# Memory keys before the tokens, four-tile lag matrices, later U loads and re-split convolution taps in a two-layer hybrid decoder step

## The chip, the cores and the metric

The kernel runs on one core of a Trainium2 chip. The metric is the device time of one execution in microseconds (us), lower is better. The engines are TensorE (PE), VectorE (DVE), ScalarE (ACT), GpSimd (POOL) and SyncE (SP, whose queue issues most loads).

## The reference

One inference step of a two-layer trunk on 512 prompt positions and 8 single-token samples, width 1024. Each layer normalises the residual, makes one input projection and runs three branches from it: a diagonal complex state-space branch, a causal depthwise convolution of 31 taps, and a 4-head cross-attention to 256 memory tokens (the samples attend to cached keys and values of their own). Gates merge the branches, and an output projection is added to the residual.

```python
def mixer_layer(x, s0_re, s0_im, conv_buf, mk, mv, p):
    h = rmsnorm(x, p['norm_g'])
    u_a, z_a, u_b, z_b, q, z_x, g_a, g_b, g_x = jnp.split(h @ p['w_in'], IN_SPLITS, axis=-1)
    y_a, s_new = s5_branch(u_a, s0, ...)          # state-space scan over positions
    o_a = (glu(gelu(y_a)) * jax.nn.silu(z_a)) @ p['w_br_ssm']
    v_b = u_b[..., :E_CONV] * jax.nn.sigmoid(u_b[..., E_CONV:])
    c_b, buf_new = causal_depthwise_conv(v_b, conv_buf, p['conv_w'], p['conv_b'])
    o_b = (silu(layernorm(c_b)) * jax.nn.silu(z_b)) @ p['w_br_conv']
    prob = jax.nn.softmax(q @ mk / sqrt(128))     # mk, mv = rmsnorm(mem) @ w_k, @ w_v
    o_x = (prob @ mv * jax.nn.silu(z_x)) @ p['w_br_xatt']
    m = sigmoid(g_a) * o_a + sigmoid(g_b) * o_b + sigmoid(g_x) * o_x
    return x + m @ p['w_out'], ...
```

## The kernel before

Everything is kept with channels on partitions: tokens are 2 groups of 260 columns (256 prompt and 4 samples). Each engine runs one instruction stream written out by hand, and semaphores alone order the work between them; a DMA stands in the queue of the engine that issues it, in program order.

**Projections.** A weight of 128 output channels arrives in two halves of 256 KB (`w_st`, loaded by SP in a fixed order). ACT casts each half to a rounded high word `w_hi`, POOL subtracts to get the low word `w_lo` (L615), and PE adds three products for each piece (`split_product`, L723): high by high, high by low, low by high. The residual is split in the same way into `h_hi` and `h_lo` by DVE and ACT at the start of each layer (the split chain, L1594 and around). The unit names are v (convolution input and gate), q, u, e (gates and the like), x (gate of the attention branch), b, a.

**Start of a layer.** `first_pair` makes the two v0 tiles; `key_values(first, end)` makes the memory's keys (0 to 3) and values (4 to 7) from `memg`, the memory tokens times the norm's gain, in quarters of the contraction. In layer 0 the tokens and memory rows arrive with tokens on partitions and PE transposes them; the row factor of the norm is spread by a product with ones (`rs`). The memory norm there runs inside the split chain. In layer 1 the square sums of the new residual give `rs`.

**DVE's taps.** `convolution(i, first, end)` runs taps `first` to `end` of channel tile i as one instruction each (L1459, `cacc<-vx,cw,cacc`); a tile starts when POOL has multiplied its gate (L627, L629). The order of these calls among DVE's other work is written out by hand:

```python
convolution(0, 0, TAPS)
convolution(1, 0, 23)
...
convolution(3, 10, TAPS)
wait(dve, l, "oxT_tr", 1)
```

**Middle of a layer.** On PE: `lag_matrices(0)` (L946, products of powers that give the state-space kernel's lags), `sample_products(0)` (L906: the samples' probabilities psT with cached values), the x1 pair, `sample_products(1)`, half of e3, `turn_sample` (the sample outputs, turned from the copy `oxs` that ACT makes), half of e3, `turn_inputs(0)`, and so on to `outputs(1)` (L958, L965). ACT copies the turned psT (L1307) after the gate of x0. SP loads U, the state-space inputs re-laid through memory, with 12 DMAs between x1's two weights. `keep_lags` copies the lag products out (`kt`), `take_inputs` and `scan` run the state recurrence on DVE, `output_matrices` makes the next V.

## Time and profile before

| | us |
|---|---|
| three runs | 1156.16, 1157.31, 1158.66 (median 1157.31) |
| profiled execution | 1154.06 |
| its span | 1152.3 |
| PE busy | 1086.5 (94%) |
| DVE busy | 813.7 (71%) |
| POOL busy | 460.0 (40%) |
| PE idle before the first q product, layers 0 and 1 | 2.85 and 6.14 |
| PE idle before the sample products, layers 0 and 1 | 5.08 and 5.42 |

A busy PE is not PE at its peak, and an engine's idle time costs only where it ends on the chain that sets the end. A timeline row gives the start in the span, the duration of the group of equal neighbours, the operation with its tiles and how many instructions it holds, and in brackets the idle time before it with what ended it.

### The profile page before, as it was taken

Reading aid. Unit: us, or ns where it says so; the run is one execution under the profiler, and the core shown is the slowest. Engines: PE = TensorE matmul, PEld = TensorE weight load, DVE = VectorE, ACT = ScalarE, POOL = GpSimd, SP = SyncE. Lnnn points to the kernel's source line nnn. Section 1 sums busy time; section 2 is a strip of 40 time slices with the busy share of each in tenths; the row PEclk is TensorE's granted clock in tenths of the full one; section 3 lists DMA queues with packets and bytes.
Section 4 is the critical chain, followed back from the end, with each engine's and each line's share of the span. In section 5 each row is a group of like instructions: output and inputs, shape, how many; then the busy total and the mean of one; then the engine's idle time right before and its main releaser. Section 6 shows DMA issues by size and latency. Waiting matters only on the chain.

```text
span 1152.3 us, 20452 instructions
## 1 busy us (share of the span) xinstructions
PE 1086.5 (94%) x8274; PEld 1015.4 (88%) x8274; DVE 813.7 (71%) x1209; ACT 419.4 (36%) x714; POOL 460.0 (40%) x329
## 2 busy tenths in 40 slices
PE   3999999989999999999989799998999999999995
PEld 3658998969999999999956799896999999999994
DVE  4868888998966784444489888989996867644412
ACT  4612553324453342222433245322444445222222
POOL 2037544454433224444313845445443322444440
PEclk8899999989999999999999899999999999999997
DMA  7235516784416723445432453478432564334422
GB/s 218 80 122 153 205 56 202 193 177 115 130 56 139 200 98 120 129 129 164 138 109 75 112 202 101 137 230 180 131 115 79 115 150 153 120 122 135 131 84 74
DMA packets 225300, 155.01 MB, mean 135 GB/s; under 512 B 48690, under 2 KB 201706, under 8 KB 223142
## 3 DMA queue, kind: packets, MB, share of 16 engines
q1 hardware_dynamic: 220454, 144.14, 44.8%
q10 hardware_dynamic: 4752, 9.57, 2.3%
q8 instruction: 65, 1.06, 0.4%
q14 instruction: 29, 0.24, 0.1%
HBM read 130.38 MB, written 24.24 MB: 134 GB/s over the span
## 4 chain that ended last, share of the span: by engine, by line
PE 66%; DVE 16%; DMA 5%; SPq 2%; POOL 2%; ACT 2%; issue 1%; DVEq 0%; ACTq 0%
PE acc L723 41%; PE mp L1059 12%; DVE cacc L1459 6%; PE mp L764 3%; PE acc L1040 2%; POOL w_lo L615 2%; DMA w_st<-in_w_in 2%; PE mp L664 2%; PE mp L935 1%; PE mp L826 1%; PE mp L864 1%; DMA y_scratch<-U 1%; DVE V L1453 1%; SPq L510 1%; DVE X L1453 1%
## 5 line engine op out<-in xcount | busy, mean ns | idle before, releaser
L615 POOL TENSOR_TENSOR w_lo<-w_st,w_hi 128x512 fp32r<-128x512 f32 x288 | 439.8, 1532 | 592.7 <-ACT w_hi L1145 592.1
L1145 ACT CAST w_hi<-w_st 128x512 fp32r<-128x512 f32 x288 | 177.4, 620 | 564.3 <-PE acc L723 370.4
L723 PE MATMUL acc<-h_hi,w_hi 128*128 128x260 f32 x1600 | 329.4, 287 | 10.0 <-POOL w_lo L615 9.0
L723 PE MATMUL acc<-h_lo,w_hi 128*128 128x260 f32 x1600 | 322.5, 283 | 0.0
L723 PE MATMUL acc<-h_hi,w_lo 128*128 128x260 f32 x1600 | 321.9, 283 | 0.0
L723 PEld LDWEIGHTS acc<-h_hi,w_hi 128*128 128x128 f32 x1600 | 247.6, 189 | 20.4 <-issue 18.1
L723 PEld LDWEIGHTS acc<-h_hi,w_lo 128*128 128x128 f32 x1600 | 247.0, 189 | 0.0
L723 PEld LDWEIGHTS acc<-h_lo,w_hi 128*128 128x128 f32 x1600 | 246.8, 189 | 0.0
L1459 DVE SCALAR_TENSOR_TENSOR cacc<-vx,cw,cacc 128x512 f32<-128x512 f32 x232 | 192.8, 902 | 1.5
L1059 PE MATMUL mp<-br_hi,w_hi 128*128 128x260 f32 x384 | 77.4, 283 | 4.7 <-POOL w_lo L615 4.7
L1059 PE MATMUL mp<-br_lo,w_hi 128*128 128x260 f32 x384 | 77.3, 283 | 0.0
L1059 PE MATMUL mp<-br_hi,w_lo 128*128 128x260 f32 x384 | 77.2, 283 | 0.0
L1453 DVE TENSOR_TENSOR mj<-mp,xT 128x520 f32<-128x520 f32 x16 | 11.2, 699 | 77.0 <-PE mp L1059 75.7
L1059 PEld LDWEIGHTS mp<-br_hi,w_hi 128*128 128x128 f32 x384 | 59.0, 188 | 5.0 <-issue 5.0
L764 PE MATMUL mp<-wkv,memg 128*128 128x512 f32 x128 | 57.5, 599 | 2.8 <-DMA wkv<-in_w_v 1.2
L1059 PEld LDWEIGHTS mp<-br_hi,w_lo 128*128 128x128 f32 x384 | 59.3, 188 | 0.0
L1059 PEld LDWEIGHTS mp<-br_lo,w_hi 128*128 128x128 f32 x384 | 59.2, 189 | 0.0
L764 PEld LDWEIGHTS mp<-wkv,memg 128*128 128x128 f32 x128 | 23.4, 190 | 34.4 <-issue 26.5
L1453 DVE TENSOR_TENSOR xT<-acc,xT 128x520 f32<-128x520 f32 x16 | 11.2, 700 | 59.4 <-PE acc L723 59.4
L1453 DVE TENSOR_TENSOR X<-X,s 128x16 f32<-128x16 f32 (+9 forms) x88 | 49.8, 566 | 3.0
L723 PE MATMUL acc<-m_hi,w_hi 128*128 128x260 f32 x256 | 51.6, 283 | 0.0
L723 PE MATMUL acc<-m_lo,w_hi 128*128 128x260 f32 x256 | 51.6, 283 | 0.0
(300 smaller groups left out, 1447.6 us busy)
## 6 DMA issues: line engine op xcount, KB each, us to landing
w_st<-in_w_in SPq DMA_DIRECT2D x208, 256.0 KB, 3.3
g_scratch<-xT ACTq DMA_DIRECT2D x32, 260.0 KB, 2.7
xT<-g_scratch SPq DMA_DIRECT2D x8, 1040.0 KB, 7.0
kb<-in_cache_mem_k SPq DMA_DIRECT2D x16, 512.0 KB, 5.3
kb<-in_cache_mem_v SPq DMA_DIRECT2D x16, 512.0 KB, 4.9
w_st<-in_w_out SPq DMA_DIRECT2D x32, 256.0 KB, 2.8
x_scratch<-xT SPq DMA_DIRECT2D x2, 2080.0 KB, 7.5
xT<-x_scratch SPq DMA_DIRECT2D x4, 1040.0 KB, 6.1
```

The costliest lines, as they stand in the source:

```text
L510: sp.dma_start(yg[:, :, t // 4, (t % 4) * C:(t % 4 + 1) * C], Ug[t * H:(t + 1) * H, :, NB:YC]).then_inc(sm["y_out"], 16)
L615: pool.tensor_tensor(w_lo[:, slot, :], w_st[:, slot, :], w_hi[:, slot, :].bitcast(F32), ALU.subtract).then_inc(w_staged_free, 1)
L664: return pe.transpose(out, in_, ident[0:n, 0:n])
L723: last = pe.matmul(acc_ps[pair][:, a, 0:HC], w[:, slot, kk * P:(kk + 1) * P], x[:, k, a, :], start=(k == 0 and p == 0), stop=(k == KT - 1 ...
L764: last = pe.matmul(mp[:, 2 * (1 - i // 4) + m, :], memg[:, k, m * P:(m + 1) * P], wkv[:, i % 2, kk * E:(kk + 1) * E], start=(k == 0), stop ...
L826: last = pe.matmul(mp[:, 2 * (i % 2) + hd // 2, (hd % 2) * MEM:(hd % 2 + 1) * MEM], q[:, hd, i // 2, (i % 2) * P:(i % 2 + 1) * P], kT[:, h ...
L864: last = pe.matmul(mp[:, hd, :], vtok[:, m, hd * P:(hd + 1) * P], pT[:, hd, m, :], start=(m == 0), stop=(m == 1))
L1040: last = pe.matmul(acc_ps[j][:, a, 0:HC], w_dir[:, g, k * 2 * P + j * P:k * 2 * P + (j + 1) * P], u[:, k, a, :], start=(k == 0), stop=(k = ...
L1059: last = pe.matmul(mp[:, 2 * jj + a, 0:HC], w[:, slot, c0:c0 + P], y[:, x, k, a, :], start=(k == 0 and i == 0), stop=(k == ET - 1 and i == 2))
L1145: act.copy(w_hi[:, c % SLOTS, :], w_st[:, c % SLOTS, :]).then_inc(w_hi_done, 1)
L1453: run(dve.tensor_tensor(out, a, b, op), behind)
L1459: run(dve.scalar_tensor_tensor(out=out, in0=a, scalar=s, in1=b, op0=op0, op1=op1), behind)
```

## The change

It has five parts. (1) In layer 0 ACT's queue issues the memory rows and two key weights before anything else; PE transposes the raw memory, DVE multiplies it by the gain out of PSUM, and PE makes the key products 0 to 3 between the token transposes. The memory's row factor is applied when ACT copies keys and values out. DVE's step factors move to before the split chain. (2) In layer 1, one key product stands before the square sums instead of two, and parameter steps move one output tile earlier, the first powers (1, 2) into the output tiles and level 4 behind the split chain. (3) The lag matrices go to four 32-column tiles of PE, and `kt`, `dt`, `eye` and `dcol` take the matching shape. (4) SP loads x1's and e3's weights and the cached values 4 to 7 before U; ACT copies psT before the second half of x0's gate. (5) The taps are split at other places, with 19 taps of tile 3 between `output_matrices(1)` and `take_inputs(1)`.

```diff
 
-                if l == 0:
-                    pair("v0")
-                    sp.dma_start(mrow[:, :, :], mem_prompt[0].rearrange("(m p) d -> p m d", p=P)).then_inc(sm["mem_in"], 16)
-                    state_loads(0)
+                if l:
                     kv_load(0)
                     kv_load(1)
-                else:
-                    kv_load(0)
-                    kv_load(1)
-                    pair("v0")
+                pair("v0")
+                if l == 0:
+                    state_loads(0)
+                    kv_load(2)
+                    kv_load(3)
                 pair("v1")
...
+                for i in range(2 if l else 4, 6):
                     kv_load(i)
-                if l:
-                    half("q0", 0)
+                half("q0", 0)
                 kv_load(6)
-                if l:
-                    half("q0", 1)
+                half("q0", 1)
                 kv_load(7)
-                if l == 0:
-                    pair("q0")
                 half("q1", 0)
...
                     wait(sp, l, "kq_done", b + 5)
                     cache_load(cache_mem_v, b)
                 half("x1", 0)
+                half("x1", 1)
+                half("e3", 0)
+                for b in range(4, NB):
+                    wait(sp, l, "pvs_done", b - 3)
+                    cache_load(cache_mem_v, b)
...
@@ -465,18 +465,13 @@
                 for a in range(2):
                     sp.dma_start(Ug[0:H, :, 4 * a:4 * a + 4], ug[:, :, a, 4 * C:HC]).then_inc(sm["U_in"], 16)
                     sp.dma_start(Ug[7 * H:P, :, YC + 4 * a:YC + 4 * a + 4], ug[:, :, a, 4 * C:HC]).then_inc(sm["U_in"], 16)
-                half("x1", 1)
-                half("e3", 0)
-                for b in range(4, NB):
-                    wait(sp, l, "pvs_done", b - 3)
-                    cache_load(cache_mem_v, b)
 
...
+            def memory_turns(j):
+
+                pe.wait_ge(sm["mem_in"], 32)
+                for k in range(HK):
+                    for m in range(2):
+                        last = transpose(acc_ps[j][:, k // 2, (k % 2) * MEM + m * P:(k % 2) * MEM + (m + 1) * P],
+                                         mrow[:, m, (HK * j + k) * P:(HK * j + k + 1) * P], P)
+                last.then_inc(sm["x_tr"], 1)
...
@@ -786,17 +790,23 @@
                     last.then_inc(sm["par_tr"], 1)
 
                 if l == 0:
+                    key_values(0, 1)
+                    token_turns(0)
+                    token_turns(1)
+                    sample_turns()
+                    key_values(1, 2)
+                    token_turns(2)
+                    token_turns(3)
+                    key_values(2, 3)
+                    row_factors()
+                    key_values(3, 4)
                     pe.wait_ge(sm["x_ev"], 5)
-                    state_turns()
-                    first_pair()
-                    pe.wait_ge(sm["mem_ev"], 2)
-                    key_values(0, 4)
                 else:
-                    key_values(0, 2)
+                    key_values(0, 1)
                     square_sums()
-                    key_values(2, 4)
-                    state_turns()
-                    first_pair()
...
                         pe.sem_inc(entered, 1)
-                    for r in range(QH):
+                    for g in range(2):
                         for ri in range(2):
-                            last = pe.matmul(mp[0:2 * H, r // 4, (r % 4) * P:(r % 4 + 1) * P],
-                                             bd[:, ri, f * QH + r, :, :].rearrange("p e h -> p (e h)"),
-                                             V[:, ri, r, 0:T, :].rearrange("p t h -> p (t h)"),
-                                             start=(ri == 0), stop=(ri == 1))
+                            for j in range(4):
+                                r = 4 * g + j
+                                last = pe.matmul(mp[32 * j:32 * j + 32, 0, g * P:(g + 1) * P],
+                                                 bd[:, ri, f * QH + r, :, :].rearrange("p e h -> p (e h)"),
+                                                 V[:, ri, r, 0:T, :].rearrange("p t h -> p (t h)"),
+                                                 start=(ri == 0), stop=(ri == 1), tile_position=(0, 32 * j))
                     last.then_inc(sm["k_done"], 1)
 
...
-                    if j == 4 and l + 1 < LAYERS:
+                    if j == 3 and l + 1 < LAYERS:
                         param_turns(l + 1)
 
...
+            for m in range(2):
+                act.dma_start(mrow[:, m, :], mem_prompt[0, m * P:(m + 1) * P, :]).then_inc(sm["mem_in"], 16)
+            for i in range(2):
+                act.dma_start(wkv[:, i, :].rearrange("p (k c) -> p k c", c=E),
+                              w_k[0].rearrange("(k p) c -> p k c", p=P)[:, 2 * i:2 * i + 2, :]).then_inc(d_loaded[i], 16)
             exponents(0)
-            sines(0)
...
+            act.wait_ge(sm["mem_in"], 32)
+            for m in range(2):
+                row_squares(P, mrow[:, m, :], 5 + m)
+            for j in range(2):
+                wait(act, 0, "memg_done", HK * (j + 1))
+                act.copy(memn[:, HK * j:HK * (j + 1), :].rearrange("p k m -> p (k m)"),
+                         acc_ps[j][:, :, :].rearrange("p b c -> p (b c)")).then_inc(sm["mem_ev"], 1)
+            act.wait_ge(sm["mem_ev"], 2)
+            act.dma_start(m_dram, memn[:, :, :].rearrange("p k m -> p (k m)")).then_inc(sm["mem_out"], 16)
             for i in range(4):
...
                     wait(act, l, "kv_used", 4)
                     if l == 0:
                         act.wait_ge(sm["mem_out"], 16)
-                    act.copy(ktok[:, :, :], mp[:, 2:4, :]).then_inc(sm["kv_ev"], 1)
-
-                if l:
-                    keep_keys()
+                    for m in range(2):
+                        last = act.activation(ktok[:, m, :], mp[:, 2 + m, :], ACT.Copy, scale=stat[:, 56 + m:57 + m])
+                    last.then_inc(sm["kv_ev"], 1)
...
                 act.activation(ps[:, :], mp[0:32, 0, 0:MEM], ACT.Exp, bias=stat[0:32, 48:49], scale=SCALE,
                                accum_out=stat[0:32, 49:50]).then_inc(sm["exps_done"], 1)
                 one("x0", 0, to_z(2))
-                one("x0", 1, to_z(2))
+                ready(1, use["x0"], unit["x0"] + 1)
                 wait(act, l, "psT_tr", 1)
                 wait(act, l, "psT_clear", 1)
                 act.copy(psT[:, :, :, 0:16], mp[:, 3, 0:64].rearrange("p (m g c) -> p m g c", m=2, g=2)).then_inc(sm["psT_ev"], 1)
...
                     if l + 1 < LAYERS:
                         square(j)
+                        if j == 3:
+                            exponents(l + 1)
                         if j == 4:
-                            exponents(l + 1)
+                            sines(l + 1)
                         if j == 5:
...
+            for j in range(2):
+                dve.wait_ge(sm["x_tr"], j + 1)
+                dve.tensor_tensor(memg[:, HK * j:HK * (j + 1), :], acc_ps[j][:, :, :].rearrange("p b (k m) -> p (b k) m", m=MEM),
+                                  vec[:, 56 + HK * j:56 + HK * (j + 1)].unsqueeze(2).to_broadcast([P, HK, MEM]),
+                                  ALU.mult).then_inc(sm["memg_done"], HK)
             angles(0)
...
             dve.sem_inc(sm["dg_done"], 1)
+            step_factors(0)
...
 
-                if l == 0:
-                    step_factors(0)
-                    first_powers()
+                first_powers((1, 2, 4) if l == 0 else (4,))
                 chunk_powers()
...
                         tt(cv[:, i, 0, :, 0:4 * C], even, odd, ALU.add)
 
                 convolution(0, 0, TAPS)
-                convolution(1, 0, 23)
+                convolution(1, 0, 14)
                 scores_max(0)
                 wait(dve, l, "qrow_ev", 2)
                 tt(qrow[32:32 + NB, :], qraw[:, :], qrow[0:NB, :].bitcast(F32), ALU.subtract)
                 dve.sem_inc(sm["qlo_done"], 1)
-                convolution(1, 23, 28)
+                convolution(1, 14, 19)
                 scores_max(1)
                 probabilities(0)
-                convolution(1, 28, TAPS)
+                convolution(1, 19, 23)
                 probabilities(1)
 
                 wait(dve, l, "b_in", 64)
...
+                convolution(1, 23, 27)
                 probabilities(3)
 
...
-                    run(dve.tensor_copy(kt[:, :, :].rearrange("h q x -> h (q x)"), mp[0:2 * H, 0:2, :].rearrange("h b x -> h (b x)")))
+                    run(dve.tensor_copy(kt[:, :, :].rearrange("h q x -> h (q x)"), mp[:, 0, 0:2 * P]))
...
                 wait(dve, l, "kv_out", 32)
                 input_matrices(0)
-                convolution(2, 3, 19)
+                convolution(1, 27, TAPS)
+                convolution(2, 0, 12)
...
                 output_matrices(0)
-                convolution(2, 19, 22)
+                convolution(2, 12, 15)
...
                 dve.tensor_scalar(ps[:, :], ps[:, :], stat[0:32, 51:52], None, ALU.mult).then_inc(sm["ps_norm"], 1)
-                convolution(2, 22, TAPS)
-                convolution(3, 0, 10)
+                convolution(2, 15, 21)
                 keep_lags(0)
-                convolution(3, 10, TAPS)
+                convolution(2, 21, TAPS)
+                convolution(3, 0, 8)
                 wait(dve, l, "oxT_tr", 1)
                 for hd in range(HEADS):
                     run(dve.tensor_copy(q[:, hd, :, 4 * C:HC], mp[:, 0:2, hd * (P + 1):hd * (P + 1) + 109:36]))
                 dve.sem_inc(sm["ox_done"], 1)
+                convolution(3, 8, 12)
...
                 output_matrices(1)
+                convolution(3, 12, TAPS)
                 take_inputs(1)
                 scan(1, lambda: keep_lags(1))
...
                             add_square(l, j - 1)
+                        if j == 2:
+                            step_rows(l + 1)
                         if j == 3:
-                            step_rows(l + 1)
+                            columns(l + 1)
                         if j == 4:
-                            columns(l + 1)
+                            angles(l + 1)
                         if j == 5:
-                            angles(l + 1)
+                            step_factors(l + 1)
                         if j == 6:
-                            step_factors(l + 1)
+                            first_powers((1, 2))
                 dve.sem_inc(sm["x_full"], 1)
                 if l + 1 < LAYERS:
                     add_square(l, KT - 1)
                     dve.sem_inc(sm["sq_sum"], 1)
-                    first_powers()
```

## Rows read from the trace of the kernel before

**Rows 1.** The page: busy time of the engines, and the chain that ended last.

```profile
PE 1086.5 (94%) x8274; PEld 1015.4 (88%) x8274; DVE 813.7 (71%) x1209; ACT 419.4 (36%) x714; POOL 460.0 (40%) x329
...
PE 66%; DVE 16%; DMA 5%; SPq 2%; POOL 2%; ACT 2%; issue 1%; DVEq 0%; ACTq 0%
```

**Rows 2.** PE's timeline in layer 0: start us, duration us, what, [idle before <- its releaser].

```profile
24.29 2.05 PE L694 MATMUL mp<-dg,ones 128*128 128x128 f32 x8 [4.55 <-DVEq L1571]
...
48.41 7.11 PE L764 MATMUL mp<-wkv,memg 128*128 128x512 f32 x16 [0.37 <-ACT memg L1098]
...
93.59 0.48 PE L723 MATMUL acc<-h_hi,w_hi 128*128 128x260 f32 x2 [2.85 <-POOL w_lo L615]
```

**Rows 3.** PE's timeline at the start of layer 1.

```profile
598.40 0.77 PE L749 MATMUL acc<-h_hi,w_hi 128*128 128x260 f32 x2 [2.61 <-DVEq L1594]
...
645.44 0.77 PE L723 MATMUL acc<-h_hi,w_hi 128*128 128x260 f32 x2 [6.14 <-POOL w_lo L615]
```

**Rows 4.** PE's timeline in the middle of layer 0.

```profile
230.00 3.68 PE L946 MATMUL mp<-V,bd 128*32 128x128 f32 x32
238.76 3.64 PE L906 MATMUL mp<-kb,psT 128*32 128x512 f32 x16 [5.08 <-ACT psT L1307]
...
254.25 1.92 PE L906 MATMUL mp<-kb,psT 128*32 128x512 f32 x16
```

**Rows 5.** DVE's timeline at the start of layer 0.

```profile
43.51 0.42 DVE L1609 COPY s<-mp 128x256 f32<-128x256 f32 x1
...
71.17 0.19 DVE L1642 COPY v_last<-vx 128x32 f32<-128x32 f32 x1 [9.88 <-POOL v_s L629]
...
73.02 19.30 DVE L1459 SCALAR_TENSOR_TENSOR cacc<-vx,cw,cacc 128x512 f32<-128x512 f32 x29
...
102.71 21.35 DVE L1459 SCALAR_TENSOR_TENSOR cacc<-vx,cw,cacc 128x512 f32<-128x512 f32 x21
```

**Rows 6.** POOL's timeline: low words under the taps of channel tiles 0 and 1.

```profile
82.83 10.61 POOL L615 TENSOR_TENSOR w_lo<-w_st,w_hi 128x512 fp32r<-128x512 f32 x1 [11.76 <-ACT w_hi L1145]
...
104.01 1.29 POOL L615 TENSOR_TENSOR w_lo<-w_st,w_hi 128x512 fp32r<-128x512 f32 x1 [1.90 <-ACT w_hi L1145]
```

**Rows 7.** DVE's timeline at the start of layer 1.

```profile
583.70 1.55 DVE L1453 TENSOR_TENSOR sq<-sq 128x520 f32<-128x520 f32 x2 [0.24 <-DVE xT L1453]
...
588.61 0.57 DVE L1453 TENSOR_TENSOR tiny<-pw 128x64 f32<-128x64 f32 x2
...
590.72 0.70 DVE L1456 TENSOR_SCALAR rs<-mp 128x520 f32<-128x520 f32 x1
...
595.56 0.76 DVE L1459 SCALAR_TENSOR_TENSOR ht<-xT,vec,rs 128x520 f32<-128x520 f32 x1 [0.70 <-ACT rs L1173]
...
607.91 1.54 DVE L1593 TENSOR_TENSOR h_lo<-ht,h_hi 128x520 fp32r<-128x520 f32 x2
...
624.88 19.30 DVE L1459 SCALAR_TENSOR_TENSOR cacc<-vx,cw,cacc 128x512 f32<-128x512 f32 x29
```

**Rows 8.** Windows behind the first q product of layer 1, granted clock after the counts.

```profile
645.44:649.00 3.56, 3.56 (x16) 3.56 (x17) 0.40 (x1) 0.00 (x0) 3.56 (x3) 0.50 0.44 129
```

**Rows 9.** ACT's timeline in the middle of layer 0.

```profile
236.59 0.62 ACT L1145 CAST w_hi<-w_st 128x512 fp32r<-128x512 f32 x1 [7.55 <-DMA w_st<-in_w_in]
```

**Rows 10.** DMA issues, 242.3 to 247.5: KB each, median us from issue to landing.

```profile
w_st<-in_w_in SPq DMA_DIRECT2D x2, 256.0 KB, 8.0
```

**Rows 11.** Windows while U is loaded, last column GB/s.

```profile
225.40:235.40 10.00, 8.28 (x71) 7.83 (x70) 9.21 (x14) 3.48 (x6) 8.71 (x2) 1.00 1.22 116
```

**Rows 12.** DVE's timeline in the second half of layer 0.

```profile
333.38 1.92 DVE L1775 COPY X<-mp 64x288 f32<-64x288 f32 x4 [9.56 <-PE mp L935]
...
345.95 1.21 DVE L1733 COPY kt<-mp 32x1024 f32<-32x1024 f32 x1
...
359.49 1.92 DVE L1809 COPY X<-X 64x576 f32<-64x576 f32 x4
```

**Rows 13.** PE's timeline in the second half of layer 0.

```profile
363.59 3.74 PE L965 MATMUL mp<-X,V 128*128 128x72 f32 x32
```

157 lines of the change are left out of this document (66 added, 91 removed).

## The prediction

> **What bounds the kernel now.** I read the page first: TensorE (PE) is busy 94% of the span and the chain that ended last is two thirds PE, so the kernel is a PE stream with holes, and a change pays by closing a hole or shortening a PE stage [rows 1]. Then I read PE's timeline for idle time and its releaser. At the start of layer 0 PE stands 4.55 us for the row factors and, at the first q product, 2.85 us for a low weight word from POOL [rows 2]. At the start of layer 1 it stands 2.61 us for the first split of h and 6.14 us for such a low word [rows 3]. In the middle of a layer it stands 5.08 us for psT between the lag matrices and the sample products, which then take 3.64 us where their second half takes 1.92 [rows 4]; layer 1 repeats this. After the 6.14 us hole the granted clock is 0.50, that is 1.2 GHz, for 3.56 us, and two products take 0.77; after the 2.85 us hole at 93.59 they take 0.48 [rows 2, 3, 8]. So the longer hole costs its length and then half a clock, the shorter only its length.
>
> Next I read what stands behind those low words. VectorE (DVE) finishes 78 small operations, waits for POOL's gate and runs 29 taps of channel tile 0 without a pause, from 73.02 for 19.30 us [rows 5]. POOL's low word of 82.83 takes 10.61 us and ends only just after that run, where one under the taps of tile 1 takes 1.29 [rows 6]. Layer 1 has the same run at 624.88, and PE starts q 20.56 us later, exactly as in layer 0 (93.59 − 73.02 = 20.57) [rows 2, 3, 5, 7]. The reader is to see that q starts in either layer when the tile-0 run ends, whatever PE has done before.
>
> **Part 1, memory keys ahead of x (layer 0).** PE gets key products while it would stand waiting for x. Sixteen of their instructions take 7.11 us, so a product takes 3.55 [rows 2]. Three of them and the memory transposes now stand before the row factors. At full clock that is 10.7 us against the 4.55 us hole and the shorter ones before it; at half clock twice that. With the transposes I put the row factors at 28.7 to 32.4 instead of 24.29. Step factors (17 small operations) also move ahead of the splits: the 78 between 43.51 and 61.29 (71.17 less 9.88 idle) take 0.23 each, so 3.6 to 4 us [rows 5]. DVE's split chain then ends at about 49 (46.8 to 52.6), where it ended just before 43.51. Behind it stand 17.8 − 3.6 = 14.2 us of small operations, 0 to 3 us (I take 2) of contention with POOL (in layer 1 the stretch from the splits' end, 609.45, to the tap run at 624.88 takes 15.4 us although it holds fewer of them [rows 7]), the 1.9 us between POOL's gate and the first chained tap, and 20.57. The gate itself no longer holds DVE, since the memory norm's scalar work leaves ScalarE (ACT). So q starts at 49 + 14.2 + 2 + 1.9 + 20.6 = 87.7 instead of 93.59: −5.9 (83.5 to 92.5). PE saves about 10 us by the reordering but reaches q 8 to 10 us too early and waits there. That hole is longer than 6.14, so the half clock after it costs half of 3.56, +1.8 [rows 8]. **Term: −4.1 (−10 to +0.6).** The extra activation for each key tile on ACT is hidden by the same wait.
>
> **Part 2, start of layer 1.** One key product instead of two before the square sums lets these start 3.55 us earlier [rows 2]. On DVE the tiny power operations between the sum of squares (ends 585.25) and rs (590.72) are gone, 5.5 us [rows 7]; both paths then allow rs at about 583.8, −6.9. The splits, 595.56 to 609.45, move with it, to 602.6. PE's first pair starts at about 596 and is PE-bound. Back on DVE comes level 4 of the powers, 2.1 us (588.61 to 590.72) [rows 7]; I take 1.5 off for contention with POOL, whose work doesn't move with the splits. The tap run starts at about 618.6 and q at 639.2 instead of 645.44. The hole stays near 4 to 6 us, with its half clock. **Term: −6.2 (−7.8 to −4.6).** The parameter steps move earlier into output tiles in which DVE waits for PE, so they cost nothing; without that cover, 21 operations at 0.2 would cost 4.
>
> **Part 3, lag matrices on four column tiles.** 32 pieces of 128 columns take 3.68 us now, one tile after another [rows 4]. No row shows them four abreast. The sample products are 16 pieces of 512 columns on four tiles in 1.92; half the columns give 0.96. Bounds: 3.68 (no gain) and 0.92 (a quarter). I take 0.96, −2.7 for each of two per layer, for the first directly; the second is swallowed below.
>
> **Part 4, loads and casts in the middle.** The psT copy stands on ACT behind a cast that waits 7.55 us for the second x1 weight [rows 9], whose load stands on SP behind the U loads. The change moves that load ahead of U, and the copy ahead of the gate's second half. The 5.08 us hole goes, and with it the half clock of the sample products (3.64 to 1.92): −6.8, with the lag −9.5. What is late next: U and the second e3 weight now stand behind four cached-value loads. Before, weights behind those landed 8.0 us after issue [rows 10], some 10.5 after the sample products (an estimate for the issue waits, 0 to 4). The stretch in which U moved lasts 10 us, at 116 GB/s [rows 11]. So e3's second half lands about 20.5 us after the sample products, and its cast stands on ACT ahead of the copy that PE's turn of the sample outputs needs. PE wants that after x1 (11.9, from 242.4 to 254.25), 1.92 and half of e3 (5.9), 19.7, less 1.9 for the shorter start: +3.4 (0 to +6). U itself is needed later, so it hides.
>
> **Part 5, taps.** Fewer taps stand before ox, so PE's 0.7 us wait there goes: −0.7. But 19 taps of tile 3 now stand between the output matrices of half 1 and take_inputs(1). DVE idles 9.56 us there today [rows 12]. 19 taps take 13.3 us at the 0.67 of tile 0, and 19.3 at the 1.02 that 21 taps of tile 1 take under POOL [rows 5]; I take 17.5. That delays take_inputs(1) by 7.9. The second lag needs its buffer, and then PE needs scan(1) at 363.59 [rows 13]: 7.9 less 0.9 for the smaller kt copy (a quarter of the columns, of 1.21 us) less 2.0 of slack (the scan's copies end at 361.4, and a last small operation follows) is +5.0 (+0.8 to +7.5). This replaces the second lag's gain, because PE would wait there anyway.
>
> **Terms 3 to 5 per layer:** −9.5 + 3.4 − 0.7 + 5.0 = −1.8 (−9.3 to +3.4).
>
> The Trainium skill ("SBUF — State Buffer", Who interferes with whom) says that DVE operations with two SBUF inputs contend with POOL's reads, and that in modes with two ports whoever issues first holds the shared port pair for the whole instruction. Our tile-0 rows agree that POOL is shut out, but for a run of 29 instructions, not one; by the rule POOL would get in between taps and q would start some 10 us earlier. That is a rival below.
>
> **Sum.** −4.1 − 6.2 − 2 × 1.8 = −13.9 against the profiled execution's 1154.06 gives 1140.2. The runs' median, 1157.31, lies 3.25 above that execution, so I predict 1143.5.
>
> **Rivals.**
> (a) Every edit counts in full, since PE is the bound: the holes of rows 2 to 4 go with their half clocks (L0 −10, L1 −11, twice −13 in the middle), −47 to −51, 1106 to 1110. For it: 94% PE. Against it: q tied to the tap run in both layers [rows 5 to 7], and 19 taps in a 9.56 us hole. Chance 0.13.
> (b) POOL gets its low word between the taps, as under tile 1 (1.29) [rows 6]: both waits for q go, with their half clocks, 13 to 16 more, 1128. Against it the 10.61. Chance 0.05.
> (c) Nothing much changes: the start runs at half clock (three key products at 7.1 put the splits 8 later than I take them, so part 1 costs 4 where I took −4.1), and the 19 taps run at 1.02 (+6.9 in place of +5.0 per layer). 8.1 + 3.8 = 11.9 back: 1155.4, and up to 1159 if the lags save nothing. For it: the first products after idle do run at half pace (0.77 for two at 598.40) [rows 3]. Chance 0.12.
> (d) Slower by one mechanism: U and the second e3 weight behind 2 MB of cached values. If that weight lands later than 28 us after the sample products instead of 20.5, each layer pays 8 more, and it decides from there: 1143.5 + 16 = 1159.5, above 1157.3 from 27.4 us on. For it: U's 116 GB/s, a poor rate [rows 11]. Against it: the cached values themselves land in a few us. Chance 0.10.
>
> **How the numbers follow.** The forecast has 0.60; adding the part-term bounds in quadrature gives its own range, 1134 to 1152. 8 in 10 needs (b) and most of (c): 1128 to 1155; left out are (a), (d) and part of (c). A measurement here tells 0.2%, 2.3 us, from no change. Faster: 0.60 + 0.13 + 0.05 and a little of (c), 0.80. Same: most of (c), 0.10. Slower: (d), 0.10.
>
> **What would show it.** Right: PE still idles at the first q product in both layers with POOL's low word as releaser, the tap run of tile 0 ending just before; rs of layer 1 some 6.9 us sooner against the first key product; lag matrices near 1 us; no idle before the sample products; some 3 us before the turn of the sample outputs and some 5 at the second half's state outputs. Wrong: no idle at q (then a or b), idle at e3 beyond 10 us (d), row factors after 33 (c).

## The result, and the profile after

The changed kernel takes 1161.51 us (median of 14 runs, 1157.73 to 1175.75) where the kernel before took 1157.70 on the same chips (1156.16 to 1159.18). The ratio is 1.0027, with a 95% interval of 1.0017 to 1.0037: 0.27% slower, where 1143.5, a faster kernel, was forecast. The execution first profiled was the outlier of 1175.75 (the other thirteen end at 1164.88), so the rows of the change come from a second profiled one, of 1158.96.

The page, first part and chain, which answer to [rows 1]:

```profile
PE 1089.9 (94%) x8274; PEld 1022.9 (88%) x8274; DVE 821.8 (71%) x1209; ACT 415.8 (36%) x709; POOL 445.5 (39%) x329
...
PE 48%; DVE 35%; SPq 5%; DMA 4%; issue 3%; POOL 3%; ACT 2%; DVEq 0%; ACTq 0%
```

PE is as busy as before, but the chain that ended last now runs through DVE for 35% of the span (16% before). PE's timeline at the two starts, beside [rows 2, 3]:

```profile
34.95 1.05 PE L707 MATMUL acc<-dg,ones 128*128 128x128 f32 x8
36.47 3.70 PE L768 MATMUL mp<-wkv,memg 128*128 128x512 f32 x8
44.15 0.77 PE L755 MATMUL acc<-h_hi,w_hi 128*128 128x260 f32 x2 [1.92 <-DVEq L1605]
132.14 1.12 PE L659 MATMUL mp<-ident,pr 128*128 128x128 f32 x4 [2.74 <-DVEq L1637]
...
585.17 1.67 PE L776 MATMUL mp<-sq,ones 128*128 128x260 f32 x4 [3.36 <-DVEq L1955]
599.40 0.49 PE L755 MATMUL acc<-h_hi,w_hi 128*128 128x260 f32 x2
643.89 0.77 PE L729 MATMUL acc<-h_hi,w_hi 128*128 128x260 f32 x2 [5.44 <-POOL w_lo L610]
```

PE's timeline in the middle of the layers, beside [rows 4, 13], with one row (431.95) from the last products of layer 0:

```profile
225.80 1.08 PE L958 MATMUL mp<-V,bd 128*32 128x128 f32 x32
226.70 1.90 PE L916 MATMUL mp<-kb,psT 128*32 128x512 f32 x16
252.11 1.97 PE L659 MATMUL mp<-ident,oxs 128*128 128x128 f32 x8 [4.01 <-ACT oxs L1341]
335.76 1.30 PE L958 MATMUL mp<-V,bd 128*32 128x128 f32 x32 [4.31 <-issue]
388.56 0.48 PE L729 MATMUL acc<-h_hi,w_hi 128*128 128x260 f32 x2 [1.92 <-ACT z L1293]
431.95 0.68 PE L1071 MATMUL mp<-br_hi,w_hi 128*128 128x260 f32 x2 [2.33 <-POOL w_lo L610]
...
860.58 5.66 PE L977 MATMUL mp<-X,V 128*128 128x72 f32 x32 [1.07 <-ACT X L1352]
911.21 5.20 PE L970 MATMUL mp<-U,Mt 128*128 128x72 f32 x32 [2.33 <-DMA Mt<-k_scratch]
916.20 7.04 PE L977 MATMUL mp<-X,V 128*128 128x72 f32 x32
```

The 5.08 us hole ahead of the sample products is gone and the lag matrices take 1.08. In its place stand holes that the kernel before did not have there, or had shorter: the turn of the sample outputs (4.01; 3.71 in layer 1), the second lag (4.31), the gate (1.92), X (1.07) and Mt (2.33).

The granted clock behind the holes, from windows (length; busy us and count of PE, PEld, DVE, ACT, POOL; granted clock, DMA share, GB/s), beside [rows 8]:

```profile
252.10:260.00 7.90, 7.89 (x44) 7.89 (x45) 3.40 (x8) 2.96 (x4) 2.81 (x3) 0.63 0.68 146
335.76:340.00 4.24, 4.24 (x46) 3.86 (x47) 4.04 (x8) 2.33 (x3) 0.00 (x0) 0.60 0.00 0
911.00:927.00 16.00, 15.79 (x82) 15.79 (x83) 6.84 (x16) 5.87 (x11) 4.99 (x4) 0.57 0.54 137
```

PE is busy in nearly all of each window, and yet the mean granted clock is 0.57 to 0.63: most of each window ran at the lower of the clock's two levels, 1.2 GHz. Added up from the first pair to the last transposes of xT, where every microsecond at half clock counts half and holes are taken out, the two executions divide so:

| us | first pair | PE work at full clock | PE idle | lost by half clock | last transposes |
|---|---|---|---|---|---|
| before | 30.89 | 1060.04 | 34.11 | 8.69 | 1133.73 |
| after | 44.15 | 1030.92 | 36.11 | 27.43 | 1138.61 |

So 29.1 us of PE work left this stretch, but the stretch starts 13.3 later, because the keys and the memory's transposes now stand ahead of the first pair; idle time is 2.0 longer, and 18.7 more went to the half clock (56.8 us at 1.2 GHz instead of 24.2, idle time within them included). −29.1 + 13.3 + 2.0 + 18.7 is the +4.9 of this execution.

These are single executions and not typical ones: over its span the one of the kernel before had a mean granted clock of 0.980 and the one of the change 0.970. The mean clock of many more runs is on record. The time lost is estimated here as (1 − clock) × span of each run (± is the standard error of a mean; the last three kernels are experiments of the next section):

| us, mean of the runs | runs | clock | lost by half clock | the rest of the time |
|---|---|---|---|---|
| before | 92 | 0.9775 | 26.0 ± 0.4 | 1132.0 |
| change | 13 | 0.9725 | 31.9 ± 1.2 | 1129.4 |
| part 3 undone | 11 | 0.9789 | 24.4 ± 0.8 | 1135.1 |
| twelve taps earlier | 6 | 0.9785 | 24.7 ± 1.4 | 1124.1 |
| holes filled | 12 | 0.9758 | 28.1 ± 0.9 | 1136.1 |

On the mean, then, the change loses 5.9 us more to the half clock than the kernel before, not 18.7, and the rest of its time is only 2.6 shorter.

### The profile page after: what moved, and what is told of

Read it like the earlier page. It is cut to its first block, busy times and chain, and to the rows that moved or that the text cites. A ratio compares the mean times of both kernels' runs of the same rounds, so it can differ in the third digit from the quotient of the medians.

```text
span 1174.0 us, 20455 instructions
## 1 busy us (share of the span) xinstructions
PE 1093.2 (93%) x8274; PEld 1025.6 (87%) x8274; DVE 810.4 (69%) x1209; ACT 416.1 (35%) x709; POOL 460.1 (39%) x329
## 4 chain that ended last, share of the span: by engine, by line
PE 53%; DVE 28%; SPq 5%; DMA 5%; POOL 4%; issue 2%; ACT 2%; DVEq 0%; ACTq 0%
PE acc L729 28%; PE mp L1071 12%; DVE cacc L1457 6%; DVE s L1451 4%; POOL w_lo L610 4%; DVE X L1451 3%; PE mp L768 3%; PE acc L1052 2%; DVE wt L1451 2%; PE acc L755 2%; SPq L464 2%; DMA w_st<-in_w_in 2%; DVE qk L1451 2%; DVE sK L1754 2%; DVE V L1451 2%
## 5 line engine op out<-in xcount | busy, mean ns | idle before, releaser
L729 PE MATMUL acc<-h_hi,w_hi 128*128 128x260 f32 x1600 | 334.5, 291 | 18.8 <-POOL w_lo L610 15.0
L729 PE MATMUL acc<-h_lo,w_hi 128*128 128x260 f32 x1600 | 326.1, 286 | 0.0
L729 PE MATMUL acc<-h_hi,w_lo 128*128 128x260 f32 x1600 | 325.9, 286 | 0.0
L729 PEld LDWEIGHTS acc<-h_hi,w_hi 128*128 128x128 f32 x1600 | 252.9, 193 | 27.6 <-issue 22.8
L729 PEld LDWEIGHTS acc<-h_hi,w_lo 128*128 128x128 f32 x1600 | 251.2, 192 | 0.0
L729 PEld LDWEIGHTS acc<-h_lo,w_hi 128*128 128x128 f32 x1600 | 250.6, 191 | 0.0
L1457 DVE SCALAR_TENSOR_TENSOR cacc<-vx,cw,cacc 128x512 f32<-128x512 f32 x232 | 195.2, 914 | 2.3
L768 PE MATMUL mp<-wkv,memg 128*128 128x512 f32 x128 | 60.4, 620 | 4.2 <-DMA wkv<-in_w_v 2.2
L729 PE MATMUL acc<-m_hi,w_lo 128*128 128x260 f32 x256 | 51.5, 283 | 0.0
```

The source lines that it names most:

```text
L729: last = pe.matmul(acc_ps[pair][:, a, 0:HC], w[:, slot, kk * P:(kk + 1) * P], x[:, k, a, :], start=(k == 0 and p == 0), stop=(k == KT - 1 ...
L768: last = pe.matmul(mp[:, 2 * (1 - i // 4) + m, :], memg[:, k, m * P:(m + 1) * P], wkv[:, i % 2, kk * E:(kk + 1) * E], start=(k == 0), stop ...
L1457: run(dve.scalar_tensor_tensor(out=out, in0=a, scalar=s, in1=b, op0=op0, op1=op1), behind)
```

## The experiments

Theory at first: the change takes out the holes it aims at, but each early or late order makes a new one, and the half clock behind the new ones takes back what the shorter PE work gives. Rival: one part alone costs more than the forecast gives it (the powers between the residual adds, the late e3 weight, the 19 taps, or POOL's lock-out), and mending it brings the forecast back. Ratios below are against the kernel before, run on the same chip; "against the change" is the difference of two ratios times 1157.7 us.

**The change again, for its profile.**

> The changed kernel once more, for a profile of a typical execution. The first profile (1175.75 us) shows granted clock 0.5 for some 75 us outside the tail's usual stretch, where the kernel before shows 34. If the lost time is mostly holes that also lower the clock, this profile shows the same holes (some 10 us before the first q product, some 5 before the turn of the sample outputs, some 4 before the second lag matrices) and fewer stretches at half clock, at 1158 to 1163 us. If the clock falls without a hole before it, the stretches stay while the holes are shorter.

Measured: 1158.96. Its rows stand above.

**One part undone at a time.** Part 1 undone (keys, token transposes and row factors in the order of before; loads and ACT steps likewise):

```diff
-                    key_values(0, 1)
-                    token_turns(0)
...
-                    row_factors()
-                    key_values(3, 4)
+                    state_turns()
+                    first_pair()
+                    key_values(0, 4)
```

> The changed kernel with part 1 (memory keys ahead of x) undone. If part 1 costs time (the parameters land 6 us later behind the memory and key loads, and q waits for the tile-0 taps all the same, 3 us later than before in the first profile): 1156 to 1158, 3 to 5 below the changed kernel. If part 1 saves the 4 us that I forecast, and the loss is in the middle: 1165.

Measured: 1172.04, ratio 1.0132 (1.0112 to 1.0152). This kernel also has layer 1's first pair ahead of its last three key products, which is no part of part 1, and PE then waits for the row scale there:

```profile
599.55 0.69 PE L664 MATMUL mp<-ident,srow 128*128 128x128 f32 x2 [4.23 <-DVE rs L1592]
```

so it says little of part 1. The same with layer 1 left alone:

> The changed kernel with part 1 (memory keys ahead of x) undone and nothing else; e2 had by mistake also put the last three key products of layer 1 behind its first pair. In e1 part 1 brings layer 0 to its middle 4.2 us sooner than the kernel before, as I forecast (4.1), and in the first profile 5.1 us later, because POOL was let into the tile-0 run in one and not in the other. If it is worth some 4 us on the mean: 1165. If e2's loss was all part 1: 1172. If it is worth nothing: 1161.

Measured: 1168.31, 1.0091 (1.0078 to 1.0104). Part 1 is worth 7.4 us in the changed kernel; the other four parts by themselves cost some 10.5.

Part 2 undone (two keys first, all powers and the parameter steps where they were):

```diff
-                    key_values(0, 1)
+                    key_values(0, 2)
                     square_sums()
-                        if j == 6:
-                            first_powers((1, 2))
```

> The changed kernel with part 2 (layer 1's start) undone. My forecast gave part 2 6.2 us: 1168 if that were so. If the small operations that it moved between the last residual adds cost what they save, as the 3.36 us hole before the square sums says: 1159 to 1163.

Measured: 1164.42, 1.0042 (1.0023 to 1.0061): 1.7 slower than the change, which the two intervals do not tell from nothing. Part 3 undone (lag matrices, kt and their DMA as before):

```diff
-                                last = pe.matmul(mp[32 * j:32 * j + 32, 0, g * P:(g + 1) * P],
+                            last = pe.matmul(mp[0:2 * H, r // 4, (r % 4) * P:(r % 4 + 1) * P],
```

> The changed kernel with part 3 (lag matrices on four tiles) undone. The four lag stages take 0.9 us each in e1 where they took 3.68, 11.1 us in all. If all of it counts: 1172. If only the first of each layer counts, as I forecast (the second is swallowed by the wait for DVE): 1167. If the longer stage only fills a hole that stands there anyway: 1161.

Measured: 1158.57, 1.0004 (0.9988 to 1.002): 2.7 faster than the change, though PE has 10.6 us more to do (1041.52 at full clock against 1030.92). Its profiled execution lost 16.7 to the half clock where that of the change lost 27.4; over all runs 7.5 less is lost and the rest is 5.7 longer (table above), so the clock gave back more than the longer work cost. Part 4 undone (loads in the old order, the psT copy behind the gate's second half):

```diff
-                ready(1, use["x0"], unit["x0"] + 1)
+                one("x0", 1, to_z(2))
...
-                to_z(2)(0, 1)
```

> The changed kernel with part 4 (order of U, x1, e3 and cached values on SP, psT copy on ACT) undone. If part 4 gains 6.8 us per layer by the hole before the sample products and gives back some 7 (first profile: 1.9 and 5.2 us of new holes in layer 0, 3.7 in layer 1), this is 1161 plus or minus 4. If the new holes are only what the profiled execution's slow clock made of them, part 4 is a gain and this is 1167 or more.

Measured: 1163.46, 1.0059 (1.0037 to 1.0081), 3.7 slower than the change. The old hole is back, and longer than the 5.08 us of [rows 4] (10.12 in layer 1):

```profile
239.06 1.08 PE L916 MATMUL mp<-kb,psT 128*32 128x512 f32 x4 [8.78 <-ACT psT L1303]
```

Part 5 undone (the taps as in the kernel before):

```diff
-                convolution(3, 12, TAPS)
                 take_inputs(1)
```

> The changed kernel with part 5 (tap split) undone. If 19 taps ahead of the second state inputs cost 5 us in each layer, as forecast: 1152. If the taps cost nothing, because PE was ahead of nothing there, and the loss is at the start: 1161. A wait of 0.7 us before the turned inputs may come back in each layer.

Measured: 1163.08, 1.0048 (1.0032 to 1.0065), 2.4 slower. The lag hole is gone, but pr waits 10.79 in place of 2.74. What follows: no part undone by itself brings back the time before, part 3 apart. The parts lean on each other.

**One suspected cost taken out of the change.** The powers behind the splits again, in both layers:

```diff
-                first_powers((1, 2, 4) if l == 0 else (4,))
+                first_powers((1, 2, 4))
...
-                        if j == 6:
-                            first_powers((1, 2))
```

> The changed kernel with layer 1's first powers (levels 1 and 2) taken out of the output tiles and put behind the split chain. In the profile of e1 these 14 small operations stand on DVE between the residual adds of the last two output tiles: the last add starts at 582.57 as before, although PE's last product is done at 578.7, and PE then idles 3.36 us before the square sums. If they are what delays it, that hole goes, rs starts some 3.5 us earlier, and the time falls by 0 to 4 (the powers come back ahead of the tap run, on which q waits): 1157 to 1161. If DVE is late for another reason, the hole stays at 3.4 and the time is 1161.

Measured: 1155.72 (1146.72 to 1162.0), 0.9982 (0.9959 to 1.0005), 5.2 faster than the change. The square sums wait 1.10 where they waited 3.36:

```profile
587.76 0.49 PE L776 MATMUL mp<-sq,ones 128*128 128x260 f32 x1 [1.10 <-DVEq L1953]
```

and DVE's last residual add, which PE waits for by way of the squares, now waits for PE's last product instead of for the powers:

```profile
583.33 0.70 DVE L1451 TENSOR_TENSOR xT<-acc,xT 128x520 f32<-128x520 f32 x1 [1.25 <-PE acc L729]
```

The second e3 weight ahead of U:

```diff
+                half("e3", 1)
                 wait(sp, l, "u_out", 16)
...
-                half("e3", 1)
```

> The changed kernel with the second half of e3's weights loaded ahead of U instead of behind it. In e1 that weight landed 21.4 us after the sample products, and PE idled 4.01 and 3.71 us before the turn of the sample outputs, at half clock behind it. If U's 10 us cause this, both holes go, and the time falls by 8 to 11: 1150 to 1153. If U, now later, is missed at the state inputs, a new hole of a few us appears there and the gain is under 4.

Measured: 1152.51, 0.9953 (0.9939 to 0.9967), 8.6 faster. The waits for oxs are gone, and U's consumer waits behind it instead, with some 10 us at half clock:

```profile
262.59 0.66 PE L945 MATMUL mp<-U,wl 128*128 128x72 f32 x2 [2.49 <-ACT wl L1309]
```

Twelve of the 19 taps earlier:

```diff
-                convolution(3, 0, 8)
+                convolution(3, 0, 20)
...
-                convolution(3, 8, 12)
+                convolution(3, 20, 24)
...
-                convolution(3, 12, TAPS)
+                convolution(3, 24, TAPS)
```

> The changed kernel with 12 of the 19 taps of tile 3 moved from between the output matrices of half 1 and the second state inputs to before ox, where DVE idles some 10 us (in the first profile of after). If the 19 taps cause the holes of 4.31 us before the second lag matrices (layer 0) and the late scan, the holes go and the time falls by 5 to 10: 1151 to 1156. If DVE's idle time before ox is not there in a typical run, a hole before the turned inputs takes their place: 1161.

Measured: 1148.41, 0.9922 (0.9907 to 0.9938), 12.2 faster, the largest single gain. The second lag matrices start behind the products with no hole (335.76 in the change):

```profile
332.01 1.08 PE L958 MATMUL mp<-V,bd 128*32 128x128 f32 x32
```

Mt no longer waits either. The profiled execution lost 14.4 us to the half clock instead of 27.4, while its idle time is not shorter (38.5); over all runs 7.2 of the gain are clock and 5.3 are the rest.

Chained taps broken at every third, so that POOL gets a turn:

```diff
-                            stt(o, src, w, o, ALU.mult, ALU.add, behind=int(k < end - 1))
+                            stt(o, src, w, o, ALU.mult, ALU.add, behind=int(k < end - 1 and k % 3 != 1))
```

> The changed kernel in which every third tap waits for the end of the tap before it, so that DVE has no next tap ready at that moment. Theory: POOL is shut out because DVE always has the next tap pending when one ends; a low word that arrives in the first 2.5 us of a run gets in and so do those behind it (e1, layer 0), one that arrives later waits for the end of the run (e1, layer 1: 7.22 us after the start, 13.2 us). Then the drains let POOL in in both layers, and the hole before q in layer 1 (5.44) goes; the tile-0 run grows from 19.3 to some 30 us, so that the score products become late instead, and the time is 1157 to 1161. Rival: POOL is shut out by something that a drain does not open (addresses, priority): the low word of layer 1 still takes over 10 us, and the drains cost some 0.1 us each, 1162 or more.

Measured: 1152.81, 0.9965 (0.9952 to 0.9979), 7.2 faster. DVE's tap run of layer 1 and POOL's first low word under it, in the change and then here:

```profile
623.32 19.30 DVE L1457 SCALAR_TENSOR_TENSOR cacc<-vx,cw,cacc 128x512 f32<-128x512 f32 x29
...
630.54 17.37 POOL L610 TENSOR_TENSOR w_lo<-w_st,w_hi 128x512 fp32r<-128x512 f32 x4 [12.69 <-ACT w_hi L1148]
```

```profile
627.52 29.62 DVE L1457 SCALAR_TENSOR_TENSOR cacc<-vx,cw,cacc 128x512 f32<-128x512 f32 x29
...
634.47 1.29 POOL L610 TENSOR_TENSOR w_lo<-w_st,w_hi 128x512 fp32r<-128x512 f32 x1 [12.40 <-ACT w_hi L1148]
```

Both low words come some 7 us into the run (7.22 and 6.95). In the change four of them share 17.37 us, of which the first holds 13.2, to the run's end; with breaks the first takes 1.29, q has no hole, and the run is 10 us longer. The same break in the kernel before:

> The kernel before with every third tap drained and nothing else. If POOL's lock-out by the tile-0 run is what holds q back, the holes of 2.85 and 6.14 us before q go in both layers, part of it comes back where the longer run makes the first probabilities late (2.7 to 3.5 us as in e1): 1150 to 1155. If the lock-out is hidden by something else in the kernel before, 1157 to 1160.

Measured: 1158.55, 0.9999 (0.9987 to 1.0011). POOL's low word under the taps of tile 0, beside the 10.61 of [rows 6], and what PE waits for in layer 1 instead:

```profile
83.63 1.36 POOL L615 TENSOR_TENSOR w_lo<-w_st,w_hi 128x512 fp32r<-128x512 f32 x1 [11.59 <-ACT w_hi L1145]
```

```profile
692.41 0.90 PE L664 MATMUL mp<-ident,pr 128*128 128x128 f32 x3 [5.44 <-DVEq L1632]
```

Both holes ahead of q are gone (2.85 and 6.14), and the time does not move: the longer runs make DVE late for pr by 1.75, 0.64 and 5.44. The lock-out is real, but in the kernel before this way out of it gains nothing.

**Mends together.** Powers late, e3 ahead of U, tile 3's taps as 14, 8 and 9, broken runs, and the first key weights issued behind the parameter loads:

```diff
+            wait(act, 0, "p_in", 160)
             for i in range(2):
                 act.dma_start(wkv[:, i, :].rearrange("p (k c) -> p k c", c=E),
```

> The changed kernel with all mends: first powers behind the splits, e3's weights ahead of U, tile 3's taps spread 14, 8, 9 about ox and before the second state inputs, every third tap drained, and ACT's two key-weight loads at the start held until the parameters have landed. If the holes are independent, as e5 to e8 have them (1155.7, 1152.5, 1148.4, 1152.8 against 1161.5), their gains add to some 33 and the parameters bring 2 to 4 more: 1125 to 1130. If they share slack (DVE becomes the bound as soon as PE stops waiting), 1138 to 1146.

Measured: 1148.33, 0.9922 (0.9909 to 0.9934), no faster than the taps alone. PE's holes are now DVE's:

```profile
133.50 0.90 PE L659 MATMUL mp<-ident,pr 128*128 128x128 f32 x3 [5.45 <-DVEq L1638]
```

and layer 1's pr, wt and X wait 2.86, 2.92 and 2.61. The same with taps of tiles 1 and 2 later as well:

```diff
-                convolution(1, 0, 14)
+                convolution(1, 0, 10)
...
-                convolution(3, 12, TAPS)
+                convolution(3, 22, TAPS)
```

> As e9, with three to four taps of tile 1 moved from ahead of the first scores to behind, and those of tile 2 behind the samples' softmax. In e5 to e8 PE idles 2.7 to 3.5 us at the first transposed probabilities because DVE comes late with them when the tile-0 run grows to 30 us. If that is DVE's order, the hole goes and the time falls 2 to 6 below e9. If DVE is full there anyway, the hole moves to the samples' probabilities, and the time is that of e9.

Measured: 1148.57, 0.9929 (0.9909 to 0.9949). The wait for pr falls from 5.45 to 0.56 (layer 0), and those for wt (layer 0) and X (layer 1) grow from 2.76 and 2.61 to 3.72 and 6.66: taps moved out of one wait land in the next. The first of these two kernels without breaks, with the keys as pairs in layer 1 and the parameter steps a tile earlier, the powers (1, 2) among them instead of behind the splits:

```diff
-                    key_values(0, 1)
+                    key_values(0, 2)
...
-                    if j == 3 and l + 1 < LAYERS:
+                    if j == 2 and l + 1 < LAYERS:
```

> The changed kernel with the holes taken away one by one and nothing that adds to DVE: e3's weights ahead of U, tile 3's taps 14, 8, 9, key weights at the start behind the parameters, two key products before layer 1's square sums as before, and the parameter steps one output tile earlier still, so that the powers stand in tiles where DVE waits. No drains. If the holes and their clock are the loss, below e7: 1135 to 1145. If DVE's load sets the pace once the holes are gone, as e9 suggests: 1146 to 1150.

Measured: 1154.79, 0.9957 (0.9936 to 0.9978). New holes at wl (3.29, twice) and at the parameter turns (2.86). Powers late and taps earlier alone:

> The changed kernel with the mends of e5 (first powers behind the splits) and e7 (12 of the 19 taps of tile 3 earlier) together. They are in different stages, and DVE has no more to do: if holes simply cost their length and clock, the gains add, 1155.7 and 1148.4 against 1161.5 give 1142 to 1144. If what one mend saves is given back elsewhere, 1147 to 1150, as e9 with all of them.

Measured: 1147.27 (1141.3 to 1151.84), 0.9902 (0.9879 to 0.9925), the fastest median: 14.5 ahead of the change and 11.3 ahead of the kernel before. The two gains (5.2 and 12.2) would add to 17.4; what the powers bring on top of the taps, 2.3, is not clear of noise. Taps earlier with the lag matrices as before:

> e7 (12 of the 19 taps of tile 3 earlier) with part 3 undone: lag matrices on one column tile, 11 us more of PE's work. If the four-tile lag matrices were worthless in e15 only because the second of each layer waited for DVE behind the taps, they are worth 5 to 11 here: 1153 to 1159. If the clock takes their gain back here too: 1147 to 1150.

Measured: 1150.29, 0.9928 (0.9908 to 0.9948), the same as with four column tiles (0.9922): their 11 us of PE work show in neither kernel.

**Holes filled with work, for the clock.** The second half of the sample products three times and of the state inputs twice, 14.7 us more on PE by repeating them:

```diff
-                sample_products(1)
+                sample_products(1, 3)
...
-                state_inputs(1)
+                state_inputs(1, 2)
```

> The changed kernel with work added: the second sample products are made three times (3.84 us more) and the state inputs of half 1 twice (3.5 us more), in both layers, with the same values, just ahead of the holes of about 4 us. If the loss is the clock that falls after a hole, and the holes' ends are set by the late weight and by DVE's 19 taps, PE fills them at no cost and keeps its clock: 4 to 10 below the changed kernel, 1152 to 1157, although 14.7 us of work are added. If the length of the holes is all that counts, nothing changes: 1161. If PE is what sets the end there, up to 14.7 longer: 1165 to 1176.

Measured: 1164.83, 1.0046 (1.0026 to 1.0067), 2.2 slower than the change, which the two intervals do not tell from nothing, so most of the 14.7 us are absorbed. The profiled execution lost 25.2 to the half clock, but it has the lowest clock of the twelve (0.972). Over all of them 3.8 less is lost than in the change and the rest is 6.7 longer: filling the holes bought back some of the clock, and less than the filling cost. In the profiled execution the longest stretch at half clock stands elsewhere now, behind a 2.08 us hole at Mt, with PE busy all through:

```profile
357.60:374.70 17.10, 17.10 (x82) 17.10 (x82) 4.83 (x15) 5.93 (x11) 4.95 (x4) 0.50 0.53 134
```

## Why the prediction was wrong, step by step

**Part 1: the size right by luck.** Forecast −4.1, the row factors at 28.7 to 32.4, PE held at q by POOL. Measured −4.2 at the first lag matrices, but with the row factors at 34.95 and the first pair at 44.15. PE's first transposes waited for the parameters until 12.49 (6.58 before; 7.21 where the mends put the key weights behind them), and a key product for its weights. q did not wait here. POOL's low word came 1.26 us after the tap run began and got in:

```profile
77.29 1.30 POOL L610 TENSOR_TENSOR w_lo<-w_st,w_hi 128x512 fp32r<-128x512 f32 x1 [12.09 <-ACT w_hi L1148]
```

The forecast's own path was late: the split chain ended at 55.21 (49 forecast, 52.6 at most) and the tap run began at 76.03 (67.1 by its sum), so that q behind that run would have come 3 us later than before and not 5.9 earlier. It did in the first profiled execution: there the low word came 2.88 us after the start and, with the three behind it, took 21.70 (the first 17.54), with a hole of 9.78 at q (96.63) and +5.1 at the first lag. Of the thirteen traces that have part 1 and unbroken taps only that one has q behind the run of layer 0; in the other twelve POOL got in. So "q starts when the tile-0 run ends" fell in layer 0 (in layer 1 it held in twelve of the thirteen). What rival (b) said, POOL between the taps, came about in layer 0, but without its price: the 29 taps then take 30.65 instead of 19.30 and pr waits 2.74 with a half clock behind. The sign of rival (c), row factors after 33, came as well, but not by its half clock: the key product of 36.47 takes 3.70.

**Part 2: the step that failed.** It said that DVE's small operations between the sum of squares and rs were gone, that both paths then allow rs at about 583.8, and that the parameter steps "cost nothing". DVE's timeline of the changed kernel at the end of layer 0, beside [rows 7]:

```profile
577.27 0.41 DVE L1451 TENSOR_TENSOR tiny<-pw 128x16 f32<-128x16 f32 x2
...
582.35 0.18 DVE L1467 COPY pw<-tiny 128x32 f32<-128x32 f32 x1
582.57 0.70 DVE L1451 TENSOR_TENSOR xT<-acc,xT 128x520 f32<-128x520 f32 x1
583.51 1.55 DVE L1451 TENSOR_TENSOR sq<-sq 128x520 f32<-128x520 f32 x2 [0.24 <-DVE xT L1451]
...
586.88 0.70 DVE L1454 TENSOR_SCALAR rs<-mp 128x520 f32<-128x520 f32 x1 [1.82 <-PE mp L776]
```

The powers run from 577.27 to 582.5 and the last residual add follows without idle time, while PE has finished its products and one key and stands 3.36 us for the squares. They did not vanish, they moved ahead of the add that PE waits for. In the kernel before, the parameter steps held the same add, up to 582.76:

```profile
582.76 0.70 DVE L1453 TENSOR_TENSOR xT<-acc,xT 128x520 f32<-128x520 f32 x1
```

So the forecast's own [rows 7] have the sum of squares end at 585.25, later than the 583.8 that it gives rs, and nothing in its sum brings the add forward. rs came at 586.88, 3.8 earlier than before where 6.9 was forecast. Behind the splits (end at 605.61, 609.45 before) level 4 of the powers and what stands with it took 2.3 more where 0.6 was put, so the tap run and q came 1.6 earlier where 6.2 was forecast. Part of that is older: layer 1's first key product, in the kernel before and then in the change, already is 0.9 ahead:

```profile
579.08 7.03 PE L764 MATMUL mp<-wkv,memg 128*128 128x512 f32 x16
```

```profile
578.22 3.60 PE L768 MATMUL mp<-wkv,memg 128*128 128x512 f32 x8
```

Part 2 itself gained 0.7 in this execution. Undone, it costs 1.7, not clear of noise; with the powers back behind the splits the change is 5.2 faster.

**Part 3: right in the row, nothing in the time.** 1.08 was measured for 0.96; −2.7 in each layer was to follow from it. Undone, the kernel is no slower (1.0004), and with the taps mended it makes no difference either (0.9928 and 0.9922).

**Part 4: right.** The psT hole went and the sample products run at full clock; at the second products PE is 9.8 ahead, counted from the first lag matrices, where −9.5 was said. What was late next was named too: ACT's second e3 cast waits for its load and stands ahead of the copy. ACT's timeline, beside [rows 9]:

```profile
249.21 0.62 ACT L1148 CAST w_hi<-w_st 128x512 fp32r<-128x512 f32 x1 [13.49 <-DMA w_st<-in_w_in]
250.03 0.62 ACT L1148 CAST w_hi<-w_st 128x512 fp32r<-128x512 f32 x1 [0.20 <-DMA w_st<-in_w_in]
...
251.06 1.00 ACT L1341 COPY oxs<-mp 128x1024 f32<-128x1024 f32 x1
```

The weight landed at 249.96, 21.4 us after the first sample products ended at 228.6 (20.5 forecast from [rows 10, 11]); PE waits 4.01 and 3.71 (3.4 forecast; the terms printed for it, 20.5 less 19.7 and plus 1.9, give 2.7). The half clock behind it (0.63 for the 7.90 us of the window) was in no term.

**Part 5: the size right in layer 0, its followers not priced.** DVE's timeline where it idled 9.56 us before [rows 12]; 19 taps took 15.56 (17.5 forecast; 16.80 in layer 1):

```profile
316.41 15.56 DVE L1457 SCALAR_TENSOR_TENSOR cacc<-vx,cw,cacc 128x512 f32<-128x512 f32 x19
```

The second lag waits 4.31 and loses 1.7 by the clock (+5.0 forecast); the profile names no releaser, but the hole goes when the taps do. In layer 1 it is X and Mt that wait, and the X products run at half pace: the window from 911 to 927. Twelve of the taps ahead of take_inputs(1) were too many: moved away, they give 12.2.

**The sum, and the second step that failed: the clock.** Forecast and measured, stage by stage, in this execution: start of layer 0 −4.1 and −4.2; middle of layer 0 −1.8 and +1.5; from there to the middle of layer 1 −6.2 and +1.0, of which 1.7 is the half clock behind the row of 431.95, ahead of part 2; middle of layer 1 −1.8 and +4.8; the end 0 and +1.8, again behind the last products. The forecast's rule was that the longer hole costs half a clock and the shorter only its length. By it a half clock was charged once, +1.8, and 1.7 was taken off at each layer's sample products, −1.6 in all. Behind the holes of 3.4 and 5.0 us that it added to each layer it put nothing, though its own [rows 4] have the products at half pace behind a hole of 5.08. The rows show half clock behind holes of 1.07 to 5.44.

How much of the miss that is differs by execution. In the profiled one 18.7 more went to the clock, about the whole miss of 18.8. Over all runs it is 5.9 where −1.6 was forecast, 7.5 of a miss of some 17; the other 10 are time that was to be saved and was not (the rest is 2.6 shorter where 12.3 was forecast). The 0.27% by which it is slower is none of the rivals named: (d) put all of it on the e3 weight, whose mend is worth 8.6, but so are the taps worth 12.2 and the powers 5.2. What fell with the experiments is the view that any of these by itself is the cause. They don't add (8.6, 12.2, 5.2 and 7.2 together gave 12.2); in the rows of the mended kernel it is DVE that ends the waits.

**What stays open.** That the lost time stands at half clock is in the rows. That holes bring it was argued at first, and filling two of them gave only part of it back. All twenty traces together say more. Between the first pair and the last transposes, 153 of 156 stretches at half clock begin in a hole of PE or at most 4 us behind one. Counted so, half clock comes with 57 of 57 holes of 4 us and more, 33 of 35 of 3 to 4, 54 of 72 of 2 to 3, 14 of 48 of 1 to 2 and 2 of 50 of 0.5 to 1. What decides for a hole of 2 to 3 us is open (next section). Why a low word gets in or not by when it comes is not known either; only that breaks in the run let it in. Part 1's two outcomes (−4.2 and +5.1) come from the same program. The division into clock and rest was profiled in two executions of the change only; for the other runs it is the estimate from the mean clock.

## What to carry to other kernels

Work taken off PE is only worth what the next waiting engine lets through: here 11 us less PE work (the lag matrices) gave nothing, and moving 12 taps gave 12.2. Before small operations are put "into a hole" of an engine, look whether that engine's next result is the one that PE waits for; a hole at which DVE waits for PE turns round as soon as PE is early. Price every new hole of 2 us or more with its possible half clock, one by one, and expect mends not to add.

## What the runs showed of the hardware that was not expected

POOL under an unbroken run of DVE's two-input operations has two outcomes. Sixteen of the traces have unbroken runs of 29 taps, 32 runs in all. In 13 of them the first low word came 0.49 to 2.57 us after the run's start, took 1.28 to 1.90, and all later ones got in too, the run growing from 19.30 to between 30.6 and 31.7. In the other 19 it came 2.67 to 11.86 us after the start and stood until the run's end, for 8.6 to 17.8 us. The two ranges do not overlap, but time from the start is not all of it. POOL's operation 0.1 us into the six-tap run of tile 2 stood 5.1 us, past that run's 4.05; and in the 19-tap run of the change (316.41) low words that came after 3.72 and 6.46 us took 1.63 and 1.27, while one after 12.90 stood 3.79, past the run's end. The Trainium skill ("SBUF — State Buffer", Who interferes with whom) says that issue order decides who blocks, not the shape of the operations, and that in DVE's modes with two ports the first to issue has the shared ports for the whole instruction. The traces agree in that the same two operations have either outcome. That the hold outlasts one instruction, and ends with the run, they show against it, and POOL came second in all 32 runs, so coming second alone does not shut it out.

The same hole comes with and without the half clock. The last products of either layer wait 2.33 us for POOL's low word in both kernels. In the kernel before:

```profile
434.64 0.47 PE L1059 MATMUL mp<-br_hi,w_hi 128*128 128x260 f32 x2 [2.33 <-POOL w_lo L615]
```

and the window behind it:

```profile
434.64:440.00 5.36, 5.36 (x45) 5.36 (x46) 2.77 (x3) 0.62 (x1) 1.29 (x1) 1.00 0.18 52
```

There the clock stays at 1.00; in the change the pair of 431.95 takes 0.68 in place of 0.47, and the clock falls to 0.50 behind it in both layers:

```profile
431.95:437.00 5.05, 5.05 (x29) 5.05 (x30) 1.06 (x2) 0.36 (x1) 0.00 (x1) 0.66 0.19 55
```

PE did the same products ahead of it in both. The twenty traces have 40 such holes, of 2.3 to 2.7 us: 29 come with half clock and 11 without, in the change both with it, with the powers late both without.
